# Two attentions, the loading of x and the spatial matmuls of a four-mixer transformer kernel: four changes of order and division

## The chip, the cores and the metric

The program runs on one core of a Trainium2 chip. Five engines work on their own instruction streams and meet at semaphores: TensorE (PE, its weight loads shown apart as PEld), VectorE (DVE), ScalarE (ACT), GpSimd (POOL) and SyncE (SP), which here only issues transfers. ACT issues transfers too. The metric is the device time of one execution in microseconds (us), as the median of several.

## The reference

Two blocks, one after the other, on 512 tokens (4 tiles of 128) of width 1024, all in float32. What the change touches is cut out here:

```python
# first block, second layer: causal attention with a forget bias, 16 heads of width 64
s = einsum('bhqd,bhkd->bhqk', q_blk, k) * scale + cum_blk[..., None] - cum[:, :, None, :]
s = where(key_pos[None, :] <= qpos[:, None], s, -inf)
p = softmax(s, axis=-1);  o = einsum('bhqk,bhkd->bhqd', p, v)

# second block, first layer: full attention, 16 query heads, 4 key heads
s = einsum('bqkgd,bskd->bkgqs', q_blk, k) * scale
p = softmax(s, axis=-1);  o = einsum('bkgqs,bskd->bqkgd', p, v)

# second block, second layer: the spatial product of the gated MLP, 16 groups of 192 columns
v = einsum('gpq,bnqgc->bnpgc', w_s, v) + b_s.T[None, None, :, :, None]
return (u * v) @ w_out
```

Around them stand a convolution and state-space mixer as the very first layer (its first product is x @ w_in), convolved and squared-ReLU feed-forwards, layer norms and modulated RMS norms.

## The kernel before

**The large products.** Every weight matrix passes in units of 512 KB through a ring of four slots. SP loads a unit (`raw`), ACT writes a rounded copy (`whi`, line 595), POOL writes the remainder (`wlo`, line 537), and PE makes each product out of three matmuls: high by high, high by low, low by high (`mm3`, lines 1834 to 1836). A unit of the first stage takes 24 such matmuls of 512 columns. The activations are split in the same way: `xhi` and `xlo`, each in eight blocks `k` of 128 features.

**The start.** SP issues the constants, the first four units and then 30-odd small parameter loads. ACT issues x as one transfer of 2 MB and then waits for the weight units to split them. PE waits for x and the constants, transposes x block by block into the PSUM banks 0 to 3 (`pe_xt_first`, line 1839), ACT copies each block to `xf` (line 624), and DVE makes `xhi` (line 1159) and `xlo` (line 1161) of it. The first three units are interleaved over `k`: PE takes block k of units 0, 1 and 2, then transposes block k + 4 (`pe_xt_late`), and before block 5 it transposes the table of parameters (`pe_table`). From unit 3 on one unit follows another.

**The attentions** (`pe_attn`, `act_attn`, `dve_attn`). A group g is one pair of heads and one tile of 128 queries; there are 32, four to a pair. In step g PE computes the scores of group g (lines 2163 and 2164, or 2179), transposes the two probability blocks of group g - 2 into the banks 4 and 5 (`TBANK`, line 2148), and weighs the values with group g - 3 (`weigh`, line 2121). Every fourth step it also spreads the row sums (line 2131). DVE takes the row maximum of both heads (line 1559), and ACT the two exponentials (line 860). The transposed blocks are copied from PSUM to `ptb`. In the causal attention (A = 0) ACT copies both heads of an even group (line 872) and DVE both heads of an odd one (line 1571); in the full one (A = 1) ACT copies the first head (line 870), DVE the second (line 1569). DVE does it behind the row maximum of the step. ACT does it behind the two exponentials of the step. In the causal attention the query tiles of a pair run 0, 1, 2, 3, and tile i has (i + 1) * 128 keys. PE may transpose a group only when the banks of the group before are copied.

**The spatial product** (`spatial`, line 2254). Of the 24 chunks of 128 columns, 16 lie in one group and 8 in two. A chunk in two groups is made in two pieces of 64 columns, first the four token tiles of the one piece, then the four of the other.

The order of all this is written out by hand: there is no scheduler.

Of the kernel before, what the change touches and what calls it, by code (L numbers as in the profile page):

```python
# [21 lines left out]
P = 128  # L22
# [26 lines left out]
TSLOTS = 8  # L49
LAG = 2  # L50
# [32 lines left out]
KEEP_BUSY = (0, 18, 0, 16)  # L83
NRM_COUNT = {t: NRM_ORDER.index((t, 0)) + 1 for t in range(4)}
# [40 lines left out]
def build_in(ctx, nc, a, out):  # L125
# [164 lines left out]
    x_in = sem("x_in")  # L290
# [201 lines left out]
    def _(sp):  # L492
        sp.dma_start(consts[:], a["consts"]).then_inc(consts_in, 16)
# [108 lines left out]
    def act_params(act):  # L602
        act.dma_start(xres[:], a["x"][0].rearrange("(t p) d -> p t d", p=P)).then_inc(x_in, 16)
# [4 lines left out]
    def act_table(act):  # L608
        act.wait_ge(tab_tp, 1)
# [7 lines left out]
    def act_xt(act, q, scale, bias):  # L617

        for k in range(KD):
# [3 lines left out]
            if scale is None:  # L623
                act.activation(xf[:, k % 2], ps[:, k % 4], ACT.Copy).then_inc(xt_ev, 1)
            else:
                act.activation(xf[:, k % 2], ps[:, k % 4], ACT.Identity, scale=scale(k), bias=bias(k)).then_inc(xt_ev, 1)

    def act_xbc(act):
        S = U0["xbc"]

        def tap(e, j):
            act_whi(act, S + AHEAD, e, j)
# [216 lines left out]
    def act_attn(act, A, ptb, causal, hook=None, build=None):  # L849
        B, G = 64 * A, 32 * A  # L850
        for g in range(32 + LAG):
# [10 lines left out]
            w = g - LAG  # L862
            if w >= 0 and (A or w % 2 == 0):
                N = (w % 4 + 1) * P if causal else T
                act.wait_ge(at_tp, B + 2 * w + (1 if A else 2))
                if w >= 4:
                    act.wait_ge(at_pv, G + w - 3)
                z = 2 * w % TSLOTS
                if A:
                    act.activation(ptb[:, z, 0:N], ps[:, TBANK, 0:N], ACT.Copy).then_inc(at_pt_a, 1)  # L870
                else:
                    act.activation(ptb[:, z:z + 2, 0:N], ps[:, TBANK:TBANK + 2, 0:N], ACT.Copy).then_inc(at_pt_a, 1)
# [282 lines left out]

    def dve_xt(dve, q, resid=None):
        for k in range(KD):
            dve.wait_ge(xt_ev, KD * q + k + 1)
# [384 lines left out]
    def dve_attn(dve, A, oT, ptb, causal, hook=None):  # L1543
# [9 lines left out]
        for g in range(32 + LAG):  # L1553
            if hook:
                hook(g)
            if g < 32:
                N = (g % 4 + 1) * P if causal else T
# [4 lines left out]
            if w >= 0 and (A or w % 2):  # L1562
                N = (w % 4 + 1) * P if causal else T
# [4 lines left out]
                if A:  # L1568
                    dve.tensor_copy(ptb[:, z + 1, 0:N], ps[:, TBANK + 1, 0:N]).then_inc(at_pt_d, 1)
                else:  # L1570
                    dve.tensor_copy(ptb[:, z:z + 2, 0:N], ps[:, TBANK:TBANK + 2, 0:N]).then_inc(at_pt_d, 1)
# [185 lines left out]
    def _(dve):  # L1757
# [3 lines left out]
        dve_xt(dve, 0)  # L1761
# [78 lines left out]

    def pe_xt_first(pe):
# [18 lines left out]
    def pe_xt_late(pe, q, k):  # L1860

        if q:
            pe.wait_ge(nrm_done, 8 * q)
        pe.wait_ge(xt_ev, KD * q + k - 3)
        for t in range(NT):
            ins = pe_xt_block(pe, nrm if q else xres, k, t)
        ins.then_inc(xt_tp, 1)

    def pe_table(pe):

        pe.wait_ge(tab_in, TAB_LOADS)
        pe.wait_ge(xt_ev, 8)
# [478 lines left out]
```

## Time and profile before

| what | value |
|---|---|
| median of 3 runs | 2913.88 us (2913.74 to 2915.85) |
| the profiled execution, its own time | 2914.31 us |
| its span, first to last instruction | 2912.4 us |
| PE busy | 2824.7 us, 97% |
| PE weight loads | 2307.6 us, 79% |
| DVE, ACT, POOL busy | 46%, 37%, 39% |
| mean granted TensorE clock | 0.987 of full speed |
| attentions | causal 982.5 to 1080 us, full 1595.2 to 1716 us of the span |
| spatial matmuls | between 2283 and 2415 us |

PE is the busy engine throughout, and what is left of the span is its waits. A figure in square brackets at the end of a timeline row is the time that the engine sat idle before it, with what ended the wait. A matmul's printed duration is longer than its step, since matmuls overlap: the step is read from two starting times.

### The profile page before, as it was taken

What the parts mean: (1) busy time and instruction counts of PE and PEld (TensorE: products, weight loads), DVE (VectorE), ACT (ScalarE), POOL (GpSimd) and SP (SyncE); (2) the same over time, 40 slices, a digit from 0 to 9 for tenths busy, and PEclk for the clock granted to TensorE, in tenths of its full rate; (3) what the DMA queues carried; (4) which work ended last, traced back from release to release, by engine and by line L of the source; (5) the groups of instructions that cost most, each with busy time, mean ns of one, the idle gap of its engine ahead of it and who ended that gap; (6) DMA issues with size and microseconds to landing.
All of it is one profiled execution on the core that took longest, in us unless ns stands there. A gap on an engine that the chain in (4) does not pass through costs nothing.

```text
span 2912.4 us, 37540 instructions
## 1 busy us (share of the span) xinstructions
PE 2824.7 (97%) x13692; PEld 2307.6 (79%) x13692; DVE 1342.1 (46%) x1516; ACT 1074.1 (37%) x1516; POOL 1147.2 (39%) x472
## 2 busy tenths in 40 slices
PE   7999799999999989999989999999999999999999
PEld 6787588888878768888877678888888888888887
DVE  4432837885345456886347653112232633331132
ACT  4323144333344334334343644233342323432332
POOL 3443043444434203544424214444534434434443
PEclk9999799999999999999999999999999999999999
DMA  5332025773233103873323013333233222333332
GB/s 148 87 95 79 0 80 163 250 229 94 87 96 93 51 8 114 262 238 115 101 65 99 1 44 86 94 101 101 94 123 106 82 80 94 101 85 96 101 100 73
DMA packets 319106, 299.90 MB, mean 103 GB/s; under 512 B 16205, under 2 KB 250905, under 8 KB 318873
## 3 DMA queue, kind: packets, MB, share of 16 engines
q1 hardware_dynamic: 303992, 235.66, 27.4%
q10 hardware_dynamic: 15008, 62.80, 6.2%
q8 instruction: 72, 1.18, 0.2%
q14 instruction: 34, 0.27, 0.0%
HBM read 296.30 MB, written 2.11 MB: 102 GB/s over the span
## 4 chain that ended last, share of the span: by engine, by line
PE 43%; issue 38%; POOL 15%; DVE 2%; ACT 1%; POOLq 0%; DVEq 0%; ACTq 0%
POOL wlo L537 15%; PE ps L1946 7%; PE ps L1948 7%; PE ps L1947 7%; PE ps L1834 6%; PE ps L1835 5%; PE ps L1836 5%; PE ps L2254 1%; DVE rowst L1559 1%; PE ps L2121 1%; PE ps L2148 1%; ACT pbuf L860 1%; PE ps L1970 0%; PE ps L1972 0%; PE ps L1971 0%
## 5 line engine op out<-in xcount | busy, mean ns | idle before, releaser
L537 POOL TENSOR_TENSOR wlo<-raw,whi 128x1024 fp32r<-128x1024 f32 x444 | 1121.9, 2530 | 1726.2 <-ACT whi L595 1725.9
L1834 PE MATMUL ps<-xhi,whi 128*128 128x512 f32 x1824 | 715.7, 392 | 7.9 <-DVE xlo L1161 6.2
L1836 PE MATMUL ps<-xhi,wlo 128*128 128x512 f32 x1824 | 710.8, 390 | 0.0
L1835 PE MATMUL ps<-xlo,whi 128*128 128x512 f32 x1824 | 710.6, 390 | 0.0
L595 ACT ACTIVATE whi<-raw 128x1024 fp32r<-128x1024 f32 x444 | 466.1, 1051 | 347.4 <-PE ps L1948 171.9
L1946 PE MATMUL ps<-whi,ahi 128*128 128x512 f32 x1184 | 463.8, 392 | 8.9 <-issue 7.8
L1948 PE MATMUL ps<-whi,alo 128*128 128x512 f32 x1184 | 462.6, 391 | 0.0
L1947 PE MATMUL ps<-wlo,ahi 128*128 128x512 f32 x1184 | 462.5, 391 | 0.0
L1834 PEld LDWEIGHTS ps<-xhi,whi 128*128 128x128 f32 x1824 | 342.9, 188 | 80.9 <-DVE xlo L1161 6.6
L1836 PEld LDWEIGHTS ps<-xhi,wlo 128*128 128x128 f32 x1824 | 342.8, 188 | 71.6
L1835 PEld LDWEIGHTS ps<-xlo,whi 128*128 128x128 f32 x1824 | 343.0, 188 | 69.4
L1946 PEld LDWEIGHTS ps<-whi,ahi 128*128 128x128 f32 x1184 | 223.6, 189 | 56.4 <-issue 8.9
L1948 PEld LDWEIGHTS ps<-whi,alo 128*128 128x128 f32 x1184 | 223.4, 189 | 46.8
L1947 PEld LDWEIGHTS ps<-wlo,ahi 128*128 128x128 f32 x1184 | 223.7, 189 | 46.3
L1350 DVE TENSOR_TENSOR alo<-hid_mlp,ahi 128x1024 fp32r<-128x1024 f32 x60 | 76.4, 1273 | 242.1 <-ACT ahi L749 242.1
L1695 DVE SCALAR_TENSOR_TENSOR hid_mlp<-ps,relu 128x512 f32 (+1 forms) x64 | 44.3, 692 | 281.3 <-ACT relu L987 281.3
L1946 PE MATMUL ps<-whi,xhi 128*128 128x512 f32 x416 | 162.9, 392 | 0.9 <-POOL wlo L537 0.7
L1948 PE MATMUL ps<-whi,xlo 128*128 128x512 f32 x416 | 161.9, 389 | 0.0
L1947 PE MATMUL ps<-wlo,xhi 128*128 128x512 f32 x416 | 161.9, 389 | 0.0
L1495 DVE SCALAR_TENSOR_TENSOR acc<-adaraw,ccol,acc 128x1536 f32<-128x1536 f32 x56 | 152.9, 2768 | 4.1 <-DMA adaraw<-in_ada_w 4.0
L749 ACT ACTIVATE ahi<-hid_mlp 128x1024 fp32r (+1 forms) x60 | 63.7, 1062 | 205.2 <-PE ps L1948 205.2
L987 ACT ACTIVATE relu<-ps 128x512 f32<-128x512 f32 x64 | 38.3, 599 | 229.3 <-PE ps L1836 229.3
(278 smaller groups left out, 2935.8 us busy)
## 6 DMA issues: line engine op xcount, KB each, us to landing
adaraw<-in_ada_w ACTq DMA_DIRECT2D x64, 768.0 KB, 6.1
raw<-in_ffn_w_up SPq DMA_DIRECT2D x88, 512.0 KB, 3.9
raw<-in_mlp_w_in SPq DMA_DIRECT2D x64, 512.0 KB, 4.0
raw<-in_mlp_w_out SPq DMA_DIRECT2D x64, 512.0 KB, 3.6
raw<-in_gmlp_w_in SPq DMA_DIRECT2D x48, 512.0 KB, 3.8
raw<-in_sc_ssm_w_in SPq DMA_DIRECT2D x44, 512.0 KB, 3.8
raw<-in_ffn_w_down SPq DMA_DIRECT2D x44, 512.0 KB, 3.6
raw<-in_fox_w_in SPq DMA_DIRECT2D x24, 512.0 KB, 3.7
```

The source lines that it names most:

```text
L537: pool.tensor_tensor(wlo[:, j], raw[:, j], whi[:, j].bitcast(F32), ALU.subtract).then_inc(w_lo, 1)
L595: act.activation(whi[:, s], raw[:, s], ACT.Copy).then_inc(w_hi, 1)
L749: act.activation(ahi[:, (m0 + j) % 2], x, ACT.Copy).then_inc(a_hi, 1)
L1350: dve.tensor_tensor(alo[:, s], x, ahi[:, s].bitcast(F32), ALU.subtract).then_inc(a_lo, 1)
L1495: dve.scalar_tensor_tensor(x, adaraw[s][:], ccol[:, bass.ds(i, 1)], x, ALU.mult, ALU.add).then_inc(ada_acc, 1)
L1695: dve.scalar_tensor_tensor(hid_mlp[:, bass.ds(e, 1)], ps[:, bank_f(j):bank_f(j) + 1], 0.0, relu[:, j % 2:j % 2 + 1], ALU.max, ALU.mult).th ...
L1834: pe.matmul(out, lh, rh, start=start, stop=False)
L1835: pe.matmul(out, lh, rl, start=False, stop=False)
L1836: return pe.matmul(out, ll, rh, start=False, stop=stop)
L1946: pe.matmul(out, lh[:, k, c], wh[:, k], start=st, stop=False, skip_group_check=True)
L1947: pe.matmul(out, lh[:, k, c], wl[:, k], start=False, stop=False, skip_group_check=True)
L1948: ins = pe.matmul(out, ll[:, k, c], wh[:, k], start=False, stop=False, skip_group_check=True)
```

## The change

Four things change.

1. **The start.** x comes in halves of 512 features, each as two transfers of 512 KB (`load_x`), one issued by SP, one by ACT. The identity matrix comes first and alone, the other constants after the units. SP's order is identity, x's first half, units 0 and 1, x's second half, units 2 and 3, the other constants, the parameters. PE transposes the identity 14 times before x and 24 times behind the first four blocks (`pe_busy`, `KEEP_START`); the products are written to a bank that nobody reads. DVE takes `xhi` and `xlo` straight out of PSUM (`dve_x_first`), without ACT's copy. ACT splits four units ahead, not three. The first three units run unit by unit, in two passes over the blocks 0 to 3 and 4 to 7.
2. **The attentions' copies.** In both of them ACT now copies the first head of every group and DVE the second. ACT does it ahead of the exponentials of its step (`p_out`). PE waits for each head's copy on its own.
3. **The causal attention's query tiles** run 0, 2, 3, 1 (`QT`).
4. **The spatial pieces** alternate: for each token tile first the one piece, then the other.

```diff
+QT = (0, 2, 3, 1)
+KEEP_START = (14, 24)
 
+    def load_x(eng, t, h, arrived):
+        c = slice(h * HALF, (h + 1) * HALF)
+        eng.dma_start(xres[:, t:t + 2, c], a["x"][0].rearrange("(t p) d -> p t d", p=P)[:, t:t + 2, c]).then_inc(arrived, 16)
 
         if start == 0:
+            sp.dma_start(consts[:, 0], a["consts"][:, 0]).then_inc(ident_in, 16)
+            load_x(sp, 0, 0, xa_in)
             for e in range(RING):
                 sp_load(sp, 0, e, e, f_src(sp, w, c0, e), f_dst(e))
+                if e == 1:
+                    load_x(sp, 0, 1, xb_in)
+            sp.dma_start(consts[:, 1:4], a["consts"][:, 1:4]).then_inc(consts_in, 16)
             sp_params(sp)
...
     def act_params(act):
-        act.dma_start(xres[:], a["x"][0].rearrange("(t p) d -> p t d", p=P)).then_inc(x_in, 16)
+        load_x(act, 2, 0, xa_in)
+        load_x(act, 2, 1, xb_in)
...
         for g in range(32 + LAG):
             if hook:
                 hook(g)
+            p_out(g - LAG)
             if g < 32:
-                N = (g % 4 + 1) * P if causal else T
+                N = (QT[g % 4] + 1) * P if causal else T
                 act.wait_ge(at_max, G + g + 1)
                 for n in (2 * g, 2 * g + 1):
...
-            w = g - LAG
-            if w >= 0 and (A or w % 2 == 0):
...
-        for u in range(AHEAD):
+        for u in range(AHEAD + 1):
             act_whi(act, u, 0, 0)
-        act.wait_ge(consts_in, 32)
-        act_xt(act, 0, None, None)
...
+    def dve_x_first(dve):
+        for k in range(KD):
+            dve.wait_ge(xt_tp, k + 1)
+            dve.tensor_copy(xhi[:, k], ps[:, k % 4]).then_inc(xt_hi, 1)
+            dve.wait_ge(xt_hi, k + 1)
+            dve.tensor_tensor(xlo[:, k], ps[:, k % 4], xhi[:, k].bitcast(F32), ALU.subtract).then_inc(xt_lo, 1)
...
-            if w >= 0 and (A or w % 2):
+            if w >= 0:
...
-                if A:
-                    dve.tensor_copy(ptb[:, z + 1, 0:N], ps[:, TBANK + 1, 0:N]).then_inc(at_pt_d, 1)
-                else:
-                    dve.tensor_copy(ptb[:, z:z + 2, 0:N], ps[:, TBANK:TBANK + 2, 0:N]).then_inc(at_pt_d, 1)
+                dve.tensor_copy(ptb[:, z + 1, 0:N], ps[:, TBANK + 1, 0:N]).then_inc(at_pt_d, 1)
...
     def pe_xt_first(pe):
-        pe.wait_ge(x_in, 16)
-        pe.wait_ge(consts_in, 32)
+        pe.wait_ge(ident_in, 16)
+        pe_busy(pe, KEEP_START[0])
+        pe.wait_ge(xa_in, 32)
...
+        pe_busy(pe, KEEP_START[1])
...
-        if q is not None:
+        if q == 0:
+            for h in range(2):
+                for e in range(3):
+                    if h == 0:
+                        pe.wait_ge(w_lo, e + 1)
+                    elif e == 2:
+                        pe_table(pe)
+                    wh, wl = parts(e)
+                    for k in range(4 * h, 4 * h + 4):
+                        if e == 0:
+                            pe.wait_ge(xt_lo, k + 1)
+                        ins = mm3(pe, ps[:, bank_f(e)], wh[:, k], wl[:, k], xhi[:, k], xlo[:, k], k == 0, k == KD - 1)
+                    if h:
+                        ins.then_inc(unit_done, 1)
+                    elif e == 0:
+                        for k in range(4, KD):
+                            pe_x_late(pe, k)
...
-            for r0, r1, g in gm_pieces(cc):
-                for t in range(NT):
+            for t in range(NT):
+                for r0, r1, g in gm_pieces(cc):
```

What stands on SP at the start of the program, before:

```order
L493 DMA consts<-in_consts 128x512
L440 DMA raw<-in_sc_ssm_w_in 128x8x128 x4
L446 DMA tabraw<-in_sc_conv_w 24x128
L446 DMA tabraw<-in_ssm_conv_w 48x128
L446 DMA tabraw<-in_ssm_conv_b 12x128
```

and in the changed kernel (`tabraw` is the parameter table, `xres` is x):

```order
L461 DMA consts<-in_consts 128x128
L456 DMA xres<-in_x 128x2x512
L442 DMA raw<-in_sc_ssm_w_in 128x8x128 x2
L456 DMA xres<-in_x 128x2x512
L442 DMA raw<-in_sc_ssm_w_in 128x8x128 x2
L467 DMA consts<-in_consts 128x384
L448 DMA tabraw<-in_sc_conv_w 24x128
```

Half of x has moved onto SP: its first quarter lies ahead of unit 0, another behind unit 1, and the parameters follow as before.

What stands on ACT at the start of the program, before:

```order
L603 DMA xres<-in_x 128x4x1024
L604 DMA onehot<-in_onehot 128x16
L595 ACT_TABLE_LOAD
L595 ACTIVATE whi<-raw 128x1024 x3
L624 ACTIVATE xf<-ps 128x512 x8
L610 ACTIVATE tab<-ps 128x512
L612 ACTIVATE tab<-ps 128x256
L614 ACTIVATE wf_hi_t<-wf_raw 128x128
L595 ACTIVATE whi<-raw 128x1024
```

and in the changed kernel:

```order
L456 DMA xres<-in_x 128x2x512 x2
L616 DMA onehot<-in_onehot 128x16
L606 ACT_TABLE_LOAD
L606 ACTIVATE whi<-raw 128x1024 x4
L623 ACTIVATE tab<-ps 128x512
L625 ACTIVATE tab<-ps 128x256
L627 ACTIVATE wf_hi_t<-wf_raw 128x128
L647 ACTIVATE cv_85<-ps,tab 128x512
L606 ACTIVATE whi<-raw 128x1024
```

The eight copies to `xf` are gone, and the fourth unit is split before the table is copied, not behind it.

What stands on ACT in the full attention, in the steps 8 to 11 (`qT` is the copy of a transposed query block, once every fourth step), before:

```order
L971 ACTIVATE qT<-ps 128x512
L860 ACTIVATE pbuf,rowst<-ps,rowst 128x512 x2
L870 ACTIVATE ptb_139<-ps 128x512
L860 ACTIVATE pbuf,rowst<-ps,rowst 128x512 x2
L870 ACTIVATE ptb_139<-ps 128x512
```

and in the changed kernel:

```order
L984 ACTIVATE qT<-ps 128x512
L872 ACTIVATE ptb_139<-ps 128x512
L884 ACTIVATE pbuf,rowst<-ps,rowst 128x512 x2
L872 ACTIVATE ptb_139<-ps 128x512
L884 ACTIVATE pbuf,rowst<-ps,rowst 128x512 x2
```

The copy of group g - 2 has moved from behind the two exponentials of group g to ahead of them.

## Rows read from the trace of the kernel before

**Rows 1.** PE's waits, whole span: waiting for whom, us in total, times, longest.
```profile
PE ps L2148 <- ACT ptb L870: 10.9, 17, 1.7
...
PE ps L2148 <- DVE ptb L1571: 3.5, 7, 1.2
```
**Rows 2.** Timeline of the start, all engines: start, duration, instructions [idle before].
```profile
10.33 3.65 PE L1839 MATMUL ps<-consts,xres 128*128 128x128 f32 x16 [10.33 <-DMA onehot<-in_onehot]
...
11.26 1.06 ACT L595 ACTIVATE whi<-raw 128x1024 fp32r<-128x1024 f32 x1 [8.15 <-DMA raw<-in_sc_ssm_w_in]
12.39 7.14 POOL L537 TENSOR_TENSOR wlo<-raw,whi 128x1024 fp32r<-128x1024 f32 x3 [11.94 <-ACT whi L595]
...
17.37 2.71 DVE L1161 TENSOR_TENSOR xlo<-xf,xhi 128x512 fp32r<-128x512 f32 x1
...
20.13 0.80 PE L1834 MATMUL ps<-xhi,whi 128*128 128x512 f32 x1 [6.16 <-DVE xlo L1161]
...
20.45 0.69 DVE L1161 TENSOR_TENSOR xlo<-xf,xhi 128x512 fp32r<-128x512 f32 x1
...
25.04 0.39 PE L1835 MATMUL ps<-xlo,whi 128*128 128x512 f32 x1
...
25.27 0.39 PE L1836 MATMUL ps<-xhi,wlo 128*128 128x512 f32 x1
...
27.93 0.40 SPq L440 DMA_DIRECT2D raw<-in_sc_ssm_w_in  x1
...
40.07 0.78 ACT L636 ACTIVATE cv<-ps,tab 128x512 f32<-128x512 f32 x1 [3.00 <-PE ps L1836]
```
**Rows 3.** Stretches of the start: length, busy (instructions), PEclk, DMA share, GB/s.
```profile
14.40:17.70 3.30, 0.00 (x0) 0.00 (x0) 1.22 (x2) 2.03 (x3) 3.30 (x3) 1.00 0.56 132
17.80:24.60 6.80, 4.47 (x12) 3.50 (x13) 5.37 (x7) 1.20 (x2) 1.73 (x1) 0.50 0.10 25
```
**Rows 4.** DMA issues: line, count, size, us from issue to landing.
```profile
xres<-in_x ACTq DMA_DIRECT2D x1, 2048.0 KB, 9.1
...
consts<-in_consts SPq DMA_DIRECT2D x1, 256.0 KB, 2.8
```
**Rows 5.** Timeline of PE, causal attention: the first scores of groups 4, 8, 12.
```profile
991.28 0.49 PE L2163 MATMUL ps<-kh,qh 128*128 128x128 f32 x2
...
1002.47 0.49 PE L2163 MATMUL ps<-kh,qh 128*128 128x128 f32 x2
...
1014.21 0.49 PE L2163 MATMUL ps<-kh,qh 128*128 128x128 f32 x2
```
**Rows 6.** Timeline of PE, the end of the causal attention.
```profile
1074.14 0.85 PE L2148 MATMUL ps<-consts,pbuf 128*128 128x128 f32 x6 [1.20 <-DVE ptb L1571]
...
1075.98 1.06 PE L2148 MATMUL ps<-consts,pbuf 128*128 128x128 f32 x8 [0.41 <-ACT ptb L872]
...
1078.37 0.88 PE L2121 MATMUL ps<-ptb,vtok 128*64 128x128 f32 x12 [0.51 <-DVE ptb L1571]
```
**Rows 7.** Timeline of the full attention, one step, PE, DVE and ACT.
```profile
1655.00 1.13 PE L2179 MATMUL ps<-kT,qT 64*128 64x256 f32 x8
...
1656.06 1.09 PE L2148 MATMUL ps<-consts,pbuf 128*128 128x128 f32 x8
1656.18 1.22 DVE L1559 TENSOR_REDUCE rowst<-ps 128x2 f32<-128x1024 f32 x1 [1.99 <-PE ps L2179]
...
1657.08 1.09 PE L2121 MATMUL ps<-ptb,v 128*64 128x128 f32 x16
...
1657.44 0.69 ACT L860 ACTIVATE pbuf<-ps,rowst 128x512 f32<-128x512 f32 x1 [1.74 <-DVE rowst L1559]
...
1658.11 1.13 PE L2179 MATMUL ps<-kT,qT 64*128 64x256 f32 x8
...
1658.78 0.59 ACT L870 ACTIVATE ptb<-ps 128x512 f32<-128x512 f32 x1
```
**Rows 8.** Timeline of PE, a spatial chunk in two pieces.
```profile
2327.60 1.58 PE L2254 MATMUL ps<-wsT,vg 128*64 128x128 f32 x16
```

More of the change, by code:

```diff
@@ L608, in act_table @@
     def act_table(act):
+        act.wait_ge(consts_in, 32)
         act.wait_ge(tab_tp, 1)
@@ L850, in act_attn, with p_out @@
         B, G = 64 * A, 32 * A
+        def p_out(w):
+            if w < 0:
+                return
+            N = (QT[w % 4] + 1) * P if causal else T
+            act.wait_ge(at_tp, B + 2 * w + 1)
+            if w >= 4:
+                act.wait_ge(at_pv, G + w - 3)
+            z = 2 * w % TSLOTS
+            act.activation(ptb[:, z, 0:N], ps[:, TBANK, 0:N], ACT.Copy).then_inc(at_pt_a, 1)
         for g in range(32 + LAG):
@@ L1556, in dve_attn @@
             if g < 32:
-                N = (g % 4 + 1) * P if causal else T
+                N = (QT[g % 4] + 1) * P if causal else T
                 dve.wait_ge(at_s, G + g + 1)
@@ L1561, in dve_attn @@
             w = g - LAG
-            if w >= 0 and (A or w % 2):
-                N = (w % 4 + 1) * P if causal else T
+            if w >= 0:
+                N = (QT[w % 4] + 1) * P if causal else T
                 dve.wait_ge(at_tp, B + 2 * w + 2)
@@ L1839, in pe_xt_block, with pe_busy @@
         return pe.transpose(ps[:, k % 4, t * P:(t + 1) * P], src[:, t, k * P:(k + 1) * P], ident)
+    def pe_busy(pe, n):
+        for _ in range(n):
+            pe.transpose(ps[:, 4, 0:P], ident, ident)
     def pe_xt_first(pe):
-        pe.wait_ge(x_in, 16)
-        pe.wait_ge(consts_in, 32)
+        pe.wait_ge(ident_in, 16)
+        pe_busy(pe, KEEP_START[0])
+        pe.wait_ge(xa_in, 32)
         for k in range(4):
@@ L1876, in pe_table, with pe_f @@
                 ins.then_inc(tab_tp, 1)
-    def pe_f(pe, name, freed, q=None, first=(), before_six=None, after=None):
+    def pe_f(pe, name, freed, q=None, first=(), after=None):
         S, n = U0[name], NUNITS[name]
@@ L1983, in pe_t_tail @@
                     pe.wait_ge(res_add, 8 * q - 3)
-                for _ in range(KEEP_BUSY[t]):
-                    pe.transpose(ps[:, 4, 0:P], ident, ident)
+                pe_busy(pe, KEEP_BUSY[t])
     def pe_t_jit(pe, name, free, head=None, q=None):
@@ L2130, in spread @@
             for i in range(NT):
-                ins = pe.transpose(ps[:, RBANK, i * P:(i + 1) * P], rdup[:, i], ident)
+                q = QT[i] if causal else i
+                ins = pe.transpose(ps[:, RBANK, q * P:(q + 1) * P], rdup[:, i], ident)
             ins.then_inc(at_r, 1)
@@ L2141, in pe_attn @@
                 pe.wait_ge(at_exp, B + 2 * w + 2)
-                if w and not A:
-                    pe.wait_ge(at_pt_a if w % 2 else at_pt_d, (w + 1) // 2)
                 for b in range(2):
-                    if w and A:
-                        pe.wait_ge(at_pt_d if b else at_pt_a, 16 + w)
-                    for c in range(w % 4 + 1 if causal else NT):
+                    if w:
+                        pe.wait_ge(at_pt_d if b else at_pt_a, G + w)
+                    for c in range(QT[w % 4] + 1 if causal else NT):
                         ins = pe.transpose(ps[:, TBANK + b, c * P:(c + 1) * P],
@@ L2251, in spatial @@
                 pe.wait_ge(gm_z, cc - 3)
-            for r0, r1, g in gm_pieces(cc):
-                for t in range(NT):
+            for t in range(NT):
+                for r0, r1, g in gm_pieces(cc):
                     ins = pe.matmul(ps[r0:r1, cc % 4, t * P:(t + 1) * P], vg[:, cc, t * P + r0:t * P + r1], wsT[:, g],
@@ L2332, in _ @@
         pe_f(pe, "mu1", lambda i, j: (mlp_done, i * 4 + (j + 29)), q=7, first=((res_add, 56),))
-        pe_t_jit(pe, "md1", free=lambda h: ((xt_ev, 64),) if h == 0 else ((mlp_done, 64),))
+        pe_t_jit(pe, "md1", free=lambda h: ((xt_ev, 56),) if h == 0 else ((mlp_done, 64),))
 def kernel(**inputs):
```

70 lines of the change are left out of this document (30 added, 40 removed).

## The prediction

> **What bounds the kernel now.** I read the page first: the span of 2912.4 us is almost all PE, busy 97% of it, so a change is worth what it takes out of PE's waits or PE's own work. The list of PE's waits is the second view. Its largest entries inside the stages of this change are the transposes of the attentions (L2148), which wait 10.9 us in 17 pieces for ACT's copy in the full attention and 3.5 us in 7 pieces for DVE's copy in the causal one [rows 1]. The third view is the timeline of the start, where two more waits stand: 10.33 us until x and the constants are there, and 6.16 us more for `xlo` before the first product [rows 2]. The timelines of the attentions and of one spatial chunk give the rest.
>
> **The start.** Before: x's block transposes begin at 10.33. ACT splits unit 0 at 11.26, POOL's remainders run from 12.39 at 7.14 / 3 = 2.38 us each. DVE's first `xlo` starts at 17.37 and takes 2.71 us where the next takes 0.69; it ends half a microsecond after POOL's three are through at 19.53. So the first product starts at 20.13 [rows 2]. Until 24.6 it runs at half the clock [rows 3]. ACT's evacuation of unit 0 at 40.07 marks unit 0's last matmul, which therefore began 0.39 earlier; seven steps of 0.23 (25.27 - 25.04) later, at 41.3, unit 3 begins [rows 2]. I compare on that point.
>
> After: how early is the data? 2816 KB (constants, x, unit 0) had landed by 11.26. The constants took 2.8 us for their 256 KB, x 9.1 us for 2048 KB [rows 4], so about 1.9 us are fixed, and with the issue at 0.75 the stream delivers 2816 KB in 8.6 us, 327 KB per us. The identity and x's first half (1088 KB) are then there at 2.65 + 3.3 = 6.0 us. For unit 0 its own 512 KB and ACT's part of the second half come on top (2112 KB): 2.65 + 6.5 = 9.1 us. x's rows come in pieces half as long, which may cost something, so I take 9.8. Bounds: 9.1, and no gain at all, 11.26. Then one split of 1.06 and one remainder of 2.38 plus two hand-overs of 0.1 give the first product at 13.4. x is no longer in the way: 16 transposes from about 6.0 at the slow 0.22 each (3.65 / 16, [rows 2]) end at 9.5, and DVE's pairs of about 1.4 us run straight out of PSUM, the first four done by about 12.5.
>
> From there PE has 72 matmuls at 0.227 (16.3 us), 16 transposes of x at 0.12 (1.9) and 6 of the table (0.7): unit 3 begins at 32.3. POOL's remainders of units 1 and 2 come at 15.8 and about 18.2, PE asks for them at 18.0 and 20.7, so they hide. Unit 3 is split early now and hides too. Next in line is unit 4: SP issues it at 27.93 behind the parameters [rows 2], some 4 us of transfer, split and remainder make 35.6 to 36, and PE asks at 32.3 + 5.4 = 37.7. That cover is 2 us thin. The gain is 41.3 - 32.3 = 9.0 us. From below 4.5: unit 0 not earlier (1.5), the parameters late for the table (1), the half clock back for the first products (2). From above 10.
>
> The fillers. After the 16 transposes of x, and with nothing else on PE, the granted clock reads 1.00 up to 17.7, then 0.50 while PE waits and restarts [rows 3]: 2.4 GHz and 1.2 GHz. At 1.2 GHz those 16 had themselves run at 0.22 a piece. So transposes do bring the clock up here, and the 38 fillers keep PE going from the identity's arrival to within 2 us of the first product. I take the full clock for all 72 matmuls. The Trainium skill, "TensorE: Matmul & The Clock Gate", section "Part 4: PE-mode transpose", says the opposite, that a transpose does not count as PE activity for the clock; the trace does not bear that out, as the clock had risen on transposes alone. The rival below prices it.
>
> The stretched `xlo` has both inputs in SBUF. In the changed kernel one input is PSUM. No row here shows that pair beside POOL, so it may take 0.69 or 2.71; while the blocks 4 to 7 are made, PE is busy with 8 us of units 0 to 2, which hides all but about 1 us of the longer one. The Trainium skill, "SBUF — State Buffer", section "Who interferes with whom", says that a VectorE instruction with two SBUF inputs contends with a GpSimd one that reads SBUF, and one with at most one such input does not. By it the 2.0 us (2.71 - 0.69) cannot come back, and the sum stays; without it the sum would be at most 1 us higher.
>
> **The full attention.** One step without a wait is 1658.11 - 1655.00 = 3.11 us of PE [rows 7]: scores 1.06, transposes 1.02, weighing 1.03. Let the scores of step g end at E. DVE's maximum takes 1.22 and then its copy about 0.7, so the second head is free at E + 2.0. ACT's copy (0.59) now stands ahead of the exponentials; the first head's transposes are through at E + 0.7, so it ends at E + 1.4, just as the maximum arrives, and the exponentials (0.69 each) end at E + 2.8. Before, the copy ended there plus 0.6, and PE asked at E + 3.1: that is the wait. Now PE asks for the first head at E + 3.1 with 1.7 us to spare, and for the second at E + 3.6 with 1.6 us. The exponentials are asked for a step later. So the added waits per head hide, and behind ACT's moved copy only the exponentials queue, with 3 us of slack. In the first eight steps something stays: at step 4 ACT has two table loads, DVE has the sums for the second query half, and I follow the chain to about 1.8 us of waits left. The gain is 10.9 - 1.8 = 9.1. Bounds: 6 (the first steps keep all theirs and one wait in four stays), 10.9.
>
> **The causal attention.** Four groups took 1002.47 - 991.28 = 11.19 us once and 1014.21 - 1002.47 = 11.74 from then on [rows 5]: the first four have no output copies on DVE yet. The 0.55 between them is the wait for DVE's two-head copy, six times over: 3.3 us. At the end three waits of 1.20, 0.41 and 0.51 stand [rows 6]. With tile 1 last, not tile 3, the last exponentials and copies are short, and tile 3's lie a step earlier; I leave 0.2 of the 2.1. With one head each and the narrow tile 0 beside the wide tile 3 on DVE, the tightest point is the weighing of tile 0: behind the maximum (1.23), copy (0.3), and two output steps (0.69 each) DVE is through 3.1 us after the scores of tile 3, and PE asks at 3.25. The gain is 3.3 + 1.9 = 5.2, between 1 (the new order opens waits as large as the ones closed at six places) and 5.4. The idle 4 us and the slow clock behind the attention stay: that chain of output, split and remainder is not touched.
>
> **The spatial chunks.** 16 records on 64 columns take 1.58 us in the chunk [rows 8] and 1.09 in the weighing of the attention, where the two heads alternate between output rows 0 to 63 and 64 to 127 [rows 7]. The pieces alternate the same way now: 0.49 less, in 8 chunks 3.9 us. PE does not wait there, so it is all on the path. Bounds 0 (pieces that share the moving side differently do not overlap) and 5.
>
> **The sum.** 9.0 + 9.1 + 5.2 + 3.9 = 27.2 us off the profiled execution's 2914.31 us gives 2887.1; the median lies 0.4 lower, so 2886.7.
>
> **The rivals.**
> - The fillers do not hold the clock, and the data comes late: the start gives 5, all else holds, 2890.7. For it: PE idles almost 2 us behind the fillers. Against it: the clock stayed at 1.00 for over 3 us of idleness before [rows 3].
> - ACT's or DVE's order makes a new wait in the attentions that takes two thirds of the gain there (14.3 down to 5): 2896. For it: the margin of 0.15 us at the weighing of tile 0, and the copy of the first head that must come before the exponentials. Against it: the slack of 1.6 us or more in all the other places.
> - The spatial pieces do not overlap: 2890.6.
> - Slower: ACT's queue is in order, so a late first-head transpose holds the exponentials back. If the copy pushed them on the path in each of the 64 steps by 0.6 us (its own length) the attentions would lose 38 us in place of gaining 14.3, and the time would be 2914 - 13 + 38 = 2939. It decides only from the point at which the exponentials come more than 3 us later than reckoned. Nothing in [rows 7] comes near.
> - The start's gain is absorbed later by something that does not depend on PE (the ring of loads behind the parameters): with 9 us lost, 2895.7. Against it: behind unit 4 each unit gives a load 5.4 us of time.
>
> **How the numbers follow.** Forecast 0.60, the late start 0.12, new waits in the attentions 0.10, no overlap 0.06, absorbed start 0.06, no change in sum 0.02, slower 0.03, faster than reckoned 0.01. The range takes the first five in part: lower end 2880, with 3 us for the copies' overlap and the drain that I may have set too low, upper end 2898. What a measurement can tell from no change is about 0.2%, 6 us. Every case but two lies below that: faster 0.95, same 0.02, slower 0.03.
>
> **What would show it.** The first product starting near 13.4 and a PEclk of 1.00 from there; unit 3 starting near 32.3; no wait of `whi` for unit 4's load on PE's side. L2148's waits for ACT's copy down from 10.9 to under 2 us; four causal groups in 11.2 us everywhere; the spatial chunks of 16 records in about 1.1 us. Wrong would be first products after 15 us, a PE wait for `pbuf` or `ptb` once in four steps, or a gap before unit 4.

## The result and the profile after

| kernel | median | of runs | ratio to the kernel before, 95% interval |
|---|---|---|---|
| before | 2914.74 us | 2913.74 to 2915.85 | 1 |
| changed | 2884.88 us | 2883.41 to 2885.83 | 0.9899 [0.9887, 0.991] |

The change takes 29.9 us off the median, where the forecast was 27.2 less and a time of 2886.7 us. The profiled execution has a span of 2881.5 us (2912.4 before). PE is busy for 2821.4 us of it, 98%.

Where the time went is read best from a mark that both kernels pass equally often. I take POOL's remainders `wlo`, 444 in each, and how much earlier the n-th starts than in the kernel before, all from the profiled executions, one of each kernel. I call it the distance. Behind the start it is 8.9 us (single marks stray by 0.3 from their neighbours, so a level is read over many), ahead of the causal attention 9.8, behind that attention's output products 16.2, ahead of the full attention 16.3, behind it 27.0, at the end 30.9.

| part | forecast | measured |
|---|---|---|
| the start | 9.0 | 8.9 |
| state-space mixer behind it | 0 | 0.9 |
| causal attention and what follows it | 5.2 | 6.5 |
| full attention | 9.1 | 10.7 |
| spatial product | 3.9 | 3.9 |

The last three repeat to 0.1 us in a second profile of the changed kernel (6.5, 10.7, 3.9: experiment 10). The first two do not: seven profiled executions with the same instructions at the start stand at 7.0 to 9.2 us behind it, the most where x lands first (6.72 us), the least where it lands last (8.13).

PE's waits of the changed kernel that answer to [rows 1], whole span (waiting for whom, us in total, times, longest):

```profile
PE ps L1860 <- DMA consts<-in_consts: 2.8, 1, 2.8
PE ps L2222 <- ACT pbuf L884: 2.3, 2, 1.9
PE ps L1855 <- DMA xres<-in_x: 0.9, 1, 0.9
PE ps L2206 <- ACT pbuf L884: 0.4, 1, 0.4
PE ps L2191 <- DVE ptb L1587: 0.2, 1, 0.2
```

The transposes (L2191 now) do not wait for an ACT copy any more: 10.9 us in the full attention have become nothing. DVE's 3.5 us in the causal attention are gone too; the 0.2 in the list lies in the full one. What the full attention still waits for is the exponentials (L2222), 2.3 us, of which one wait of 1.9 stood there before. The 0.4 at L2206 is a new wait for them in the causal one.

The timeline of the start, which answers to [rows 2] (start, duration, instructions, in brackets the idle time before them and what ended it):

```profile
2.76 3.25 PE L1860 MATMUL ps<-consts 128*128 128x128 f32 x14 [2.76 <-DMA consts<-in_consts]
...
6.92 3.67 PE L1855 MATMUL ps<-consts,xres 128*128 128x128 f32 x16 [0.92 <-DMA xres<-in_x]
...
8.80 0.69 DVE L1173 TENSOR_TENSOR xlo<-ps,xhi 128x512 fp32r<-128x512 f32 x1
...
9.79 1.06 ACT L606 ACTIVATE whi<-raw 128x1024 fp32r<-128x1024 f32 x1 [6.20 <-DMA raw<-in_sc_ssm_w_in]
...
10.39 3.15 PE L1860 MATMUL ps<-consts 128*128 128x128 f32 x24
...
10.93 4.74 POOL L548 TENSOR_TENSOR wlo<-raw,whi 128x1024 fp32r<-128x1024 f32 x2 [10.47 <-ACT whi L606]
...
13.35 0.50 PE L1850 MATMUL ps<-xhi,whi 128*128 128x512 f32 x1
...
13.69 0.39 PE L1851 MATMUL ps<-xlo,whi 128*128 128x512 f32 x1
...
13.92 0.40 PE L1852 MATMUL ps<-xhi,wlo 128*128 128x512 f32 x1
...
17.59 0.69 DVE L1173 TENSOR_TENSOR xlo<-ps,xhi 128x512 fp32r<-128x512 f32 x1
...
34.78 2.40 POOL L548 TENSOR_TENSOR wlo<-raw,whi 128x1024 fp32r<-128x1024 f32 x1 [14.11 <-ACT whi L606]
...
43.59 0.78 ACT L647 ACTIVATE cv<-ps,tab 128x512 f32<-128x512 f32 x1 [0.37 <-PE ps L1852]
```

PE works almost without a gap from 2.76 on, the first product starts at 13.35, not 20.13, and its successors follow at 0.23 us, the step at the full clock. The `xlo` at 17.59 runs while POOL works (15.90 to 20.67) and takes 0.69 us. The fillers bring the clock up: PE starts them 0.21 us apart until 11.03 and 0.11 apart from 11.19 on, and up to there it had made nothing but transposes.

The end of the causal attention on PE, which answers to [rows 6]:

```profile
1060.17 1.26 PE L2191 MATMUL ps<-consts,pbuf 128*128 128x128 f32 x8
...
1062.76 1.53 PE L2165 MATMUL ps<-ptb,vtok 128*64 128x128 f32 x24
1064.22 0.65 PE L2176 MATMUL ps<-consts,rdup 128*128 128x128 f32 x4
1068.85 0.47 PE L1992 MATMUL ps<-whi,ahi 128*128 128x512 f32 x1 [3.98 <-issue]
```

None of the three waits is left. The idle 3.98 us in front of the output products are there as before. The stretch at half the clock behind them is shorter. The stretches behind the attention, changed kernel (length, then busy time (instructions) of PE, its weight loads, DVE, ACT and POOL, then PEclk, DMA share, GB/s):

```profile
972.70:1064.90 92.20, 91.79 (x704) 66.89 (x704) 53.20 (x94) 49.02 (x160) 0.00 (x0) 0.98 0.00 1
1069.30:1072.70 3.40, 3.40 (x10) 2.63 (x9) 0.58 (x1) 0.08 (x1) 2.66 (x1) 0.50 0.02 5
```

and the kernel before:

```profile
982.50:1079.30 96.80, 91.81 (x700) 66.85 (x700) 54.51 (x78) 43.30 (x144) 0.00 (x0) 0.98 0.00 1
1082.70:1089.50 6.80, 5.48 (x13) 4.35 (x14) 2.36 (x2) 1.86 (x2) 2.65 (x1) 0.50 0.15 30
```

PE does the same 91.8 us of work in the attention, in 92.2 us rather than 96.8, and the stretch at half the clock is 3.4 us long where it was 6.8.

A spatial chunk in two pieces on PE, which answers to [rows 8]:

```profile
2299.12 1.09 PE L2297 MATMUL ps<-wsT,vg 128*64 128x128 f32 x16
```

It takes 1.09 us where it took 1.58, as the prediction had it.

### The profile page after: what moved, and what is told of

Read it like the earlier page. It is cut to its first block, busy times and chain, and to the rows that moved or that the text cites. A ratio compares the mean times of both kernels' runs of the same rounds, so it can differ in the third digit from the quotient of the medians.

```text
span 2881.5 us, 37694 instructions
## 1 busy us (share of the span) xinstructions
PE 2821.4 (98%) x13730; PEld 2306.2 (80%) x13730; DVE 1341.6 (47%) x1532; ACT 1078.1 (37%) x1524; POOL 1147.8 (40%) x472
## 4 chain that ended last, share of the span: by engine, by line
PE 45%; issue 37%; POOL 16%; DVE 1%; ACT 0%; POOLq 0%; DVEq 0%; ACTq 0%
POOL wlo L548 16%; PE ps L1992 7%; PE ps L1993 7%; PE ps L1994 7%; PE ps L1850 6%; PE ps L1851 6%; PE ps L1852 6%; PE ps L2222 1%; PE ps L2165 1%; PE ps L2191 1%; PE ps L2297 1%; PE ps L2016 0%; PE ps L2018 0%; PE ps L2017 0%; PE ps L1855 0%
```

## The experiments

Each kernel was timed in rounds with the kernel before. The distances are those of POOL's remainders, as above.

**1. The start alone.** The changed kernel with the attentions (order of copies, order of tiles) and the spatial loop of the kernel before:

```diff
-            p_out(g - LAG)
...
-                N = (QT[g % 4] + 1) * P if causal else T
+                N = (g % 4 + 1) * P if causal else T
...
-            for t in range(NT):
-                for r0, r1, g in gm_pieces(cc):
+            for r0, r1, g in gm_pieces(cc):
+                for t in range(NT):
```

> The kernel before with the start alone changed (x in halves, the fillers, xhi and xlo out of PSUM, four units split early, two passes over the first three units). Theory, that the parts add up as PE waits taken out: first product near 13.4 us, unit 3 on PE near 32.4, and from there to the end the same distance of 9 to 10 us, so 2904.5 to 2906 us against 2914.7. Rival, that the changed kernel's gain in the start is partly given back by the loads behind the parameters or needs the other parts: 6 us or less, 2908.5 or more.

Measured: 2906.9 us, ratio 0.9974 [0.9964, 0.9984]. The distance behind the start is 7.0 us and 7.2 at the end: nothing later absorbs it, but the 9 to 10 of the theory were missed, and the time lies between theory and rival. It is 1.9 us less than in the changed kernel. PE's timeline of this kernel shows why:

```profile
8.13 3.68 PE L1856 MATMUL ps<-consts,xres 128*128 128x128 f32 x16 [2.01 <-DMA xres<-in_x]
11.60 3.97 PE L1861 MATMUL ps<-consts 128*128 128x128 f32 x24
15.32 0.48 PE L1851 MATMUL ps<-xhi,whi 128*128 128x512 f32 x1
```

and POOL's, of the same kernel:

```profile
11.26 4.71 POOL L548 TENSOR_TENSOR wlo<-raw,whi 128x1024 fp32r<-128x1024 f32 x2 [10.81 <-ACT whi L606]
```

x landed 1.2 us later in this execution (the same instructions; the transfers differ from one execution to the next), and the 24 fillers stand between x and the first product whatever the time. POOL had the first remainder at 11.26 + 4.71 / 2 = 13.6, so the fillers held the first product back by 1.7 us. Where x comes at 6.92, as in the changed kernel, the remainder (13.3) and the fillers' end (13.35) meet.

**2. The copies alone, tiles in the old order.** The kernel before with the new attentions and `QT = (0, 1, 2, 3)`:

```diff
+QT = (0, 1, 2, 3)
...
+            p_out(g - LAG)
             if g < 32:
...
```

> The kernel before with the attentions' copies alone changed (ACT the first head ahead of the exponentials, DVE the second, in both attentions), the causal query tiles still in the order 0 1 2 3. Theory: the full attention gives 10.9 us, the causal one 3.3 (its wait once in four steps goes), its end keeps its waits: 2900 to 2901. Rival, that the causal waits are closed by the order of the tiles and not by the division of the copies: the causal attention gives under 1 us, 2903.5.

Measured: 2897.03 us, ratio 0.9944 [0.9927, 0.996], the distance at the end 17.4 us, 6.1 of it in the causal attention and 10.8 in the full one. That is 3 us better than the 2900 to 2901 expected: in the causal attention and behind it the copies give 6.1 us and not 3.3, since most of the waits at its end go too.

**3. The spatial loop alone.**

```diff
-            for r0, r1, g in gm_pieces(cc):
-                for t in range(NT):
+            for t in range(NT):
+                for r0, r1, g in gm_pieces(cc):
```

> The kernel before with the spatial pieces alternating and nothing else. Theory: eight chunks of 0.49 us, 2910.8 against 2914.7, and chunks of 16 records in about 1.1 us. Rival: what came down at that place came from somewhere else, under 1 us here.

Measured: 2910.29 us, ratio 0.9989 [0.9979, 0.9998]. The distance grows by 3.9 us across the spatial product; the only other growth behind the start is 0.5 in the state-space mixer, where nothing differs.

The three parts give 7.0 + 16.9 + 3.9 = 27.8 us in their own stages and the whole 30.9. Of the difference of 3.1, 1.9 are the start of experiment 1, 0.9 the state-space mixer, and the rest is about what experiment 4 finds for the tile order.

**4. Old tile order in the changed kernel.**

```diff
-QT = (0, 2, 3, 1)
+QT = (0, 1, 2, 3)
```

> The changed kernel with the causal query tiles in the order 0 1 2 3 again. Theory: the waits within the attention stay closed, its end is longer by about 2 us and the clock behind it slow for longer, 1.5 us more: 2887.5 to 2888.5 against 2884.9. Rival, that the order closes the waits in every period of four: 5 us or more, from 2890.

Measured: 2884.79 us, ratio 0.9901 [0.9884, 0.9917], no difference from the changed kernel that can be told: neither the 2 us at the end nor the 1.5 behind it that the theory gave to the order. PE's timeline at its causal attention's end:

```profile
1060.77 0.55 PE L2191 MATMUL ps<-consts,pbuf 128*128 128x128 f32 x3 [0.34 <-DVE ptb L1587]
...
1062.39 1.06 PE L2191 MATMUL ps<-consts,pbuf 128*128 128x128 f32 x8 [0.49 <-ACT ptb L872]
...
1065.35 0.66 PE L2176 MATMUL ps<-consts,rdup 128*128 128x128 f32 x4
```

0.83 us of waits are left here and none in the changed kernel. But from the first scores to the last row-sum transposes the attention takes 1065.35 - 973.54 = 91.81 us, and in the changed kernel 1064.22 - 972.71 = 91.51: the new order is worth 0.3 us net. Part of the 0.83 is paid back by the wait of 0.4 for the exponentials at L2206, which this kernel does not have. The copies are worth the rest of the 5.4 that separate it from the 1079.39 - 982.51 = 96.88 us before.

**5. The copy behind the exponentials again.** Everything else of the change stays: one head each for ACT and DVE, the tile order, a wait for each head.

```diff
-            p_out(g - LAG)
             if g < 32:
...
                                    accum_out=rowst[:, 1, n:n + 1]).then_inc(at_exp, 1)
+            p_out(g - LAG)
```

> The changed kernel with ACT's copy behind the exponentials of its step again, in both attentions; the division by head stays. Theory, that the place on ACT's queue is what closed the full attention's waits: about 10 us come back there and up to 3 in the causal one, 2895 to 2898 against 2884.9, with PE's transposes waiting for ACT's copy again. Rival, that PE's separate waits or the new causal division do it: under 3 us, 2887.

Measured: 2905.49 us, ratio 0.9969 [0.9958, 0.9981], 20.6 us above the changed kernel, where the theory expected 10 to 13. Its largest wait on PE:

```profile
PE ps L2191 <- ACT ptb L872: 17.9, 26, 1.8
```

The full attention gains nothing against the kernel before (distance 5.6 ahead and behind), and the causal one is slower than before by 3.2 us (8.8 ahead, 5.6 behind). Of the 17.9 us of waits 10.9 lie in the full attention, as in the kernel before, and 7.0 in the causal one. One step in its full attention:

```profile
1645.42 0.68 ACT L883 ACTIVATE pbuf<-ps,rowst 128x512 f32<-128x512 f32 x1
...
1646.09 0.59 ACT L872 ACTIVATE ptb<-ps 128x512 f32<-128x512 f32 x1
...
1646.82 1.06 PE L2191 MATMUL ps<-consts,pbuf 128*128 128x128 f32 x8 [0.59 <-ACT ptb L872]
```

The copy is 0.59 us long and starts when the exponentials are through. PE waits 0.59. In the full attention the kernel before had already one head for each engine and a wait on PE for each (line 2148), so there the place on ACT's queue is all that the change moved, and it is worth the whole 10.7 us: from the first scores to the last row-sum transposes it takes 121.0 us in both kernels with the copy behind, 110.3 with it in front. In the causal attention three things changed: with the place it gains 5.4 us, and the division by head and the new tile order without the place lose 3. Which of these two loses it was not tried.

**6. No fillers at the start.**

```diff
-KEEP_START = (14, 24)
+KEEP_START = (0, 0)
```

> The changed kernel without the 14 and 24 filling transposes at its start. Theory, that the fillers hold the clock: the first products run at half the clock, 0.43 apart, for 3 to 4 us, and the whole is 1.7 to 2.3 us longer, 2886.6 to 2887.2. Rival, that the 16 transposes of x alone suffice or that transposes do not matter: no difference, 2884.9.

Measured: 2885.54 us, ratio 0.9901 [0.9885, 0.9918]. The distance behind the start is 6.9 us, 2.0 below the changed kernel. PE's first products:

```profile
13.87 0.80 PE L1850 MATMUL ps<-xhi,whi 128*128 128x512 f32 x1 [1.72 <-POOL wlo L548]
14.46 0.63 PE L1851 MATMUL ps<-xlo,whi 128*128 128x512 f32 x1
...
17.34 0.40 PE L1852 MATMUL ps<-xhi,wlo 128*128 128x512 f32 x1
17.57 0.39 PE L1850 MATMUL ps<-xhi,whi 128*128 128x512 f32 x1
```

They follow at 0.43 us, not 0.23, for about 3 us. So the 16 transposes of x do not suffice here. Of the 2.0 us 0.5 is the first product itself, at 13.87 and not 13.35, and about 1.5 are the slow steps. But experiment 1, with the fillers, stands at 7.0 too: where x lands late the fillers hold back about as much as they save. The median of the whole time lies only 0.7 us above the changed kernel's, which these rounds cannot tell from nothing, and below the 2886.6 of the theory; the mechanism is shown by the trace, its worth by no time.

**7. x in one piece.** ACT issues x whole again, the rest of the start is new:

```diff
-            load_x(sp, 0, 0, xa_in)
...
-                if e == 1:
-                    load_x(sp, 0, 1, xb_in)
...
-        load_x(act, 2, 0, xa_in)
-        load_x(act, 2, 1, xb_in)
+        act.dma_start(xres[:], a["x"][0].rearrange("(t p) d -> p t d", p=P)).then_inc(xa_in, 16)
...
```

> The changed kernel with x loaded whole, by ACT in one transfer of 2 MB, as before the change; the identity first, the fillers, the conversion out of PSUM and the order of the products stay. Theory, that most of the start's gain comes from the path behind the data (no copies on ACT, no VectorE instruction held up by POOL, two passes): x's transposes start near 10.2, unit 0 is split at 11.3 as before the change, the first product is near 15, and 1.5 to 2.5 us of the 9 are lost, 2886.5 to 2887.5. Rival, that the halves carry the gain: 5 us or more, 2890.

Measured: 2886.21 us, ratio 0.9904 [0.9888, 0.9921]. The timeline of PE:

```profile
9.57 3.28 PE L1851 MATMUL ps<-consts,xres 128*128 128x128 f32 x16 [3.64 <-DMA xres<-in_x]
12.64 3.19 PE L1856 MATMUL ps<-consts 128*128 128x128 f32 x24
15.59 0.48 PE L1846 MATMUL ps<-xhi,whi 128*128 128x512 f32 x1
```

x is there 2.7 us later than in halves and the first product 2.2 us later, again behind the fillers; the distance is 6.7 against 8.9 behind the start and 28.9 against 30.9 at the end. The theory holds in this pair. But the seven executions in halves have x at 6.72 to 8.13 and the first product at 13.09 to 15.32, so one execution sizes the halves only roughly, and the medians, 1.3 us apart, do not.

**8. More fillers.** 28 transposes that nobody reads behind the causal attention, and ahead of the QKV product 44 before the transposes of the first token tile and 24 behind them:

```diff
+KEEP_TAIL = (44, 24)
+KEEP_FOX = 28
...
+            if q == 4:
+                pe.wait_ge(res_add, 8 * q - 3)
+                pe_busy(pe, KEEP_TAIL[0])
...
+                if q == 4 and t == 0:
+                    pe_busy(pe, KEEP_TAIL[1])
...
+        pe_busy(pe, KEEP_FOX)
         pe_t_jit(pe, "fo", q=3,
```

> The changed kernel with fillers at two more places where PE idles before a slow clock: 28 transposes behind the causal attention (4 us idle, then 3.4 us at half the clock) and 44 and 24 in the waits of 6.2 and 3.1 us before the first transposes of the second block (then 10.2 us at half the clock). Theory, that transposes hold the clock here: PE stays at full speed, the first products behind the causal attention start 0.23 apart, 1.5 us saved there and 1 to 2 us at the other place, so 2881.5 to 2882.5 against 2884.9. Rival, that transposes do not count and the start's full clock had another reason: the slow stretches stay, 2884.9 or somewhat more.

Measured: 2883.46 us, ratio 0.9897 [0.988, 0.9913], no difference from the changed kernel that can be told. Three stretches of its trace:

```profile
1069.00:1073.00 4.00, 4.00 (x18) 3.29 (x19) 1.02 (x1) 0.52 (x1) 2.68 (x1) 1.00 0.00 0
1492.40:1502.70 10.30, 8.20 (x71) 7.75 (x72) 5.34 (x8) 7.84 (x16) 0.00 (x0) 1.00 0.00 1
1581.60:1585.00 3.40, 3.40 (x16) 2.41 (x14) 1.22 (x1) 1.69 (x6) 0.00 (x0) 0.50 0.00 0
```

and the last two in the changed kernel:

```profile
1492.40:1502.70 10.30, 5.34 (x24) 4.97 (x25) 6.67 (x12) 7.80 (x16) 0.00 (x0) 0.51 0.00 1
...
1581.60:1585.00 3.40, 2.12 (x18) 1.57 (x18) 1.81 (x2) 2.93 (x9) 0.86 (x1) 1.00 0.00 0
```

Both slow stretches that the fillers aim at are gone. The one behind the causal attention was worth 1.5 us (the distance grows from 9.7 to 17.6, and in the changed kernel from 9.8 to 16.2). The long one at 1492 was worth nothing: PE waits there for ACT's norms and DVE's `xlo`, and a faster transpose only waits longer. And 1.5 us were lost again at 1581.6, where a new stretch at half the clock begins in the full attention's first steps, behind a wait of 1.94 us that the changed kernel has too.

**9. Fillers at two places.** 28 behind the causal attention as above and 16 in the wait at 1581, none ahead of the QKV product:

```diff
+KEEP_FOX = 28
+KEEP_GQA = 16
...
+            if A and g == 2:
+                pe.wait_ge(q1_copied, 4)
+                pe_busy(pe, KEEP_GQA)
```

> The changed kernel with two more groups of transposes that nobody reads: 28 behind the causal attention and 16 between the second and third score groups of the full attention. Nothing else differs; the long idle stretch ahead of the QKV product is left as it is. Theory (such transposes keep the granted clock up wherever PE idles, and the 1.5 us that the 28 gained before were lost again because a half-clock stretch of 3.4 us appeared at 1581.6 us, behind 1.94 us of idleness in the full attention's start): no stretch at half the clock behind the causal attention nor in the full attention's start, a gain of 1.5 us against the changed kernel that lasts to the end, about 2883.4 us. Rival (the end of the first block absorbs what comes before it, so nothing arrives in the full attention): the gain is 0 from 1500 us on and the time that of the changed kernel.

**10. The changed kernel once more,** in the same rounds.

> The changed kernel itself, once more, for the comparison with the one before it in this list: 2884.9 us, with 3.4 us at half the clock behind the causal attention.

Measured: 2884.44 us (0.9899 [0.9882, 0.9915]) with the fillers of experiment 9 against 2884.2 us (0.9901 [0.9884, 0.9917]). The theory holds in its part and fails in the time. Between the marks ahead of and behind the causal attention the kernel with fillers gains 15.3 - 7.3 = 8.0 us, the changed kernel in the same rounds 15.4 - 9.0 = 6.4. Through the full attention both gain 10.7, so nothing is lost there. But the kernel with fillers came into the attention 1.7 us behind, from a part of the program that is the same in both: 0.4 behind the start, the rest in the state-space mixer, where its mean clock from 270 to 370 us was 0.73 and the changed kernel's 0.76 in both executions. Differences of this size come and go between executions, and no kernel of these beats the changed one by more than that.

**11. The other operand of `xlo` from PSUM.** The kernel before, where the first eight `xlo` read the transposed block and not ACT's copy:

```diff
-            dve.tensor_tensor(xlo[:, k], xf[:, k % 2], xhi[:, k].bitcast(F32), ALU.subtract).then_inc(xt_lo, 1)
+            lo_src = ps[:, k % 4] if q == 0 else xf[:, k % 2]
+            dve.tensor_tensor(xlo[:, k], lo_src, xhi[:, k].bitcast(F32), ALU.subtract).then_inc(xt_lo, 1)
...
+        else:
+            pe.wait_ge(xt_lo, k - 3)
...
+            pe.wait_ge(xt_lo, 6)
```

The two waits on PE keep a bank until it has been read.

> The kernel before, where DVE takes the other operand of the first eight xlo from PSUM and not from ACT's copy in SBUF. Nothing else changes. Theory (the first xlo took 2.71 us because both operands were in SBUF while GpSimd worked): the first xlo takes 0.69 us, it ends about 2.0 us sooner, the first product starts near 18.1 us and not at 20.13, and the time falls by at most 2.0 us to about 2912.7, less if the rest of the start is bound by something else. Rival (the 2.71 us have to do with the first use, or DVE simply waited for a port whatever the operand): it stays at 2.7 us, with no change in time.

Measured: 2911.41 us, ratio 0.9992 [0.9982, 1.0002], a difference that the medians cannot tell from nothing; the distance is 2.5 us behind the start and 3.1 at the end, 0.5 of it from the state-space mixer. Its timeline beside POOL:

```profile
12.36 7.17 POOL L537 TENSOR_TENSOR wlo<-raw,whi 128x1024 fp32r<-128x1024 f32 x3 [11.91 <-ACT whi L595]
...
17.34 0.69 DVE L1162 TENSOR_TENSOR xlo<-ps,xhi 128x512 fp32r<-128x512 f32 x1
...
17.95 1.86 DVE L1159 CAST xhi<-xf 128x512 fp32r<-128x512 f32 x1
18.09 0.29 PEld L1835 LDWEIGHTS ps<-xhi,whi 128*128 128x128 f32 x1 [4.52 <-DVE xlo L1162]
...
20.45 0.42 DVE L1159 CAST xhi<-xf 128x512 fp32r<-128x512 f32 x1
```

`xlo` takes 0.69 us beside POOL where it took 2.71 [rows 2], and the first product starts at 18.09. It is the operand and not the first use. The stretching has moved on to the next DVE instruction that has SBUF on both sides, a cast that takes 1.86 us beside POOL and 0.42 without.

## Why the prediction was right, point by point

**The start: right in sum and in its steps.** The first product was put at 13.4 and starts at 13.35, unit 0's data at 9.8 and it is split at 9.79, unit 3 was put at 32.3. To read unit 3: ACT's copy of unit 4 ends a wait at 43.59, so unit 4's last matmul began 0.39 earlier, and 47 steps of 0.227 before that unit 3 began, at 32.5: 8.8 us ahead of the 41.3, as the distance of 8.9 has it. x came later than reckoned, 6.92 and not 6.0, and it cost nothing, since the fillers and the remainder of unit 0 set the first product. That hides a thin place: the reckoning took the fillers for free, and they are free only if x is early. In seven executions with these instructions the distance was 7.0 to 9.2, so a forecast that is met within 0.1 is in part luck of the transfers. Nor is the sum taken apart: the halves and `xlo` were changed alone, the order of the products and the fourth unit split early were not. The cover in front of unit 4 was put at 2 us; its remainder is through at 34.78 + 2.40 = 37.2 and PE asks at 32.5 + 5.4 = 37.9, so 0.7 us were left.

**The fillers: the right mechanism, with a smaller worth.** The first products step at the full clock, where 6.80 us stood at 0.50 before [rows 3], and without the fillers they do not. The prediction leaned on the full clock up to 17.7 in [rows 3]: 16 transposes had raised it there by 14.37. In experiments 6 and 11 the same 16 were followed by no full clock before 17.20 and 21.55, where the steps change to 0.23, so these 16 alone are no sure means. Without the fillers the time hardly moves. The rule of the Trainium skill that a transpose does not count for the clock ("TensorE: Matmul & The Clock Gate", "Part 4: PE-mode transpose") is not borne out by experiment 8 either, where 28 transposes and nothing else kept the clock at 1.00 behind the causal attention.

**`xlo` beside POOL: right.** The prediction left open whether it stretches with one operand in PSUM. It does not: 0.69 us in the changed kernel and in experiment 11. "SBUF — State Buffer", "Who interferes with whom", in the Trainium skill says the same: with two inputs in SBUF a VectorE instruction contends with GpSimd's reads. Its sentence on at most one such input, as the prediction gives it, lacks the page's exception: a copy or a cast from SBUF to SBUF can contend too, in the modes that take both ports. Experiment 11 agrees: a cast with one input, in SBUF, took 1.86 us beside POOL and 0.42 without.

**The full attention: mechanism right, one term too large.** The term that was mis-sized is the residual of 1.8 us in the first eight steps, which I had followed: the waits that are new are 0.4 for the exponentials and 0.2 for DVE's copy, and 10.7 us were gained where 9.1 were forecast. The 1.94 us wait for the exponentials was there before, at the same place. The prediction speaks of added waits per head; in this attention they stood there before, and only the place of the copy is new.

**The causal attention: body right, what lies behind it wrong.** Forecast 3.3 + 1.9 = 5.2, measured 96.88 - 91.51 = 5.4. The 3.3 held nearly: four groups take 11.23 us where they took 11.74, six times over, 3.1 us. The cause of the rest was wrong, and that the sum came out is luck. I gave the drain of 1.9 to the new tile order; experiments 2 and 4 show 0.3 for the order and the rest for the copies, since with a copy on each engine and ACT's in front the old order leaves only 0.83 us of waits. The failed step is "The idle 4 us and the slow clock behind the attention stay": the idle 4 us did (3.98), the slow clock did not, 6.8 us became 3.4, with 5.48 and 3.40 us of PE's work in them. At half the clock a matmul steps 0.43 and not 0.23, so the 2.08 us less are 5 matmuls that each take 0.2 less: 1.0 us, just what the marks show between the attention's body and the products behind it (6.4 - 5.4). It goes with the copies and not with the order: 3.4 us at half the clock in the six profiled executions with ACT's copy in front and no fillers there (experiments 2 and 4 have the old order), 6.8 us in the five others, experiment 5 among them. In the kernel before the clock falls 2.7 us after PE's last transposes, in the changed one 4.4 us after. I take it that PE idled less just before; that is argued from these cases and not tried by itself.

**The spatial product: right,** 3.9 us, alone and in the whole.

**The rivals.** The late start, absorbed start and no overlap are out by the distances. Of the slower rival experiment 5 shows the mirror: there the exponentials hold the copy, and the price is 20.6 us. New waits in the changed kernel's attentions came to 0.4 us in the causal one and 0.4 and 0.2 in the full one; the list of waits shows no more.

**The 0.9 us of the state-space mixer** have no cause in the change that I can name. The instructions there are the same in all kernels, and the distance changes by anything from -1.4 (experiment 9) to +0.9 us across it. The time at half the clock differs there: the mean clock from 270 to 370 us is 0.74 in the kernel before, 0.76 in the changed one and 0.73 in experiment 9.

## What to carry to other kernels

When an in-order engine does two jobs in a step, look which of them the busiest engine asks for first and put that one in front, if the other's consumer is a step away: here taking that order back lost 20.6 of the 29.9 us, and the rest of the causal attention's change without it was slower than before by 3 us. A filler that keeps the clock up is a fixed length in front of what may be ready sooner, so it is sized by the data's arrival, and its gain is counted only up to the next wait that something else ends. For small gains compare the distance at marks of equal count, and not the total alone: the parts of a few us are plain there when the medians cannot tell them. But a profile is one execution: a stage that differs between executions of the same instructions, as the start does here by 2.2 us, needs several.

## What the runs showed of the hardware

- Transposes alone bring TensorE's clock up (changed kernel, steps of 0.21 us until 11.03 and 0.11 from 11.19 on) and hold it (experiments 8 and 9). A stretch at half the clock can move: with the clock held up at 1069 and at 1492 us, one appeared at 1581.6 us behind a wait of 1.94 us (experiment 8). Which of the two groups of fillers moved it is not shown.
- The profile's granted clock reads 1.00 for 13.4 to 17.7 us in the kernel without fillers, though its first products follow at 0.43 us, the step of half the clock. The trace has no clock record there before 17.20 us, and the view counts a time without a record as full. At 17.2 the steps change to 0.23. The row of that stretch:

```profile
13.40:17.70 4.30, 3.83 (x10) 3.08 (x11) 1.58 (x3) 1.71 (x2) 4.02 (x3) 1.00 0.82 208
```

  At the start of a program the steps between matmuls are the surer sign. In the kernel before the records begin at 14.37, so the row at 17.8 in [rows 3] is read from them.
- A cast from SBUF to SBUF on DVE took 1.86 us beside POOL and 0.42 without, a subtraction of two SBUF operands 2.71 against 0.69, and one with an operand in PSUM 0.69 in both cases.
- SP's issue of its second quarter of x, the fifth transfer on its queue, took 4.61 us at 3.22 in the changed kernel; that of the unit at 27.93 in [rows 2] took 0.40. Transfers behind it are issued that much later.

```profile
3.22 4.61 SPq L456 DMA_DIRECT2D xres<-in_x  x1
```
